# Separate evacuation lane for the key and gate tiles, and another first head, in a hybrid-layer kernel on Trainium2

## The chip, the cores and the metric

The kernel runs on one core of one Trainium2 chip. The metric is the device time of one launch in microseconds (us). The kernel before takes 2522.82 us, the median of 3 runs (2521.14 to 2523.16). Differences under some 0.2% (5 us) are about what such runs cannot tell apart.

The core has a matrix engine (TensorE, PE in the profile, with PEld its weight loads), three elementwise engines (VectorE or DVE, ScalarE or ACT, GpSimd or POOL) and queues that issue transfers (SP). Each engine runs its own instructions strictly in the order in which they were written, and engines wait for each other by semaphores.

## The reference

512 tokens of width 1024 go through two layers of one kind (gated delta rule, sliding-window attention, gated MLP) and one of another kind (a state-space branch and a pooling branch), which the change leaves alone. Of a layer of the first kind this much matters:

```python
h = rmsnorm(x, pre_mix_g)
proj = h @ w_in
(dn_q, dn_k, dn_v, dn_z, dn_b, dn_a, sw_q, sw_k, sw_v, gate_a, gate_b) = split(proj)

# delta rule, 8 heads of 128, chunks (here 128 rows on the chip)
qkv = silu(causal_conv4(concat(dn_q, dn_k, dn_v)))   # four taps
q = l2norm(q) * 128**-0.5;  k = l2norm(k)
beta = sigmoid(dn_b)
g = cumsum(-exp(a_log) * softplus(dn_a + dt_bias))   # the decay, by chunk
L = strict(beta * k @ k.T * exp(g_i - g_j));  T = inverse(1 + L)
a = (q @ k.T) * exp(g_i - g_j)
# scan over chunks: state, output o, then
o = rmsnorm(o, norm_g) * silu(dn_z)

# attention rotates the first 16 of each head's 64 columns of q and k
y = sigmoid(gate_a) * (o @ w_up_dn) + sigmoid(gate_b) * (attention @ w_up_sw)
x = x + rmsnorm(y @ w_o, post_mix_g)
x = x + rmsnorm(square(relu(rmsnorm(x, pre_mlp_g) @ w_ff1)) @ w_ff2, post_mlp_g)
```

## The kernel before

**Tiles and parts.** Everything is kept transposed: 128 features in the partitions, 512 tokens in the columns. A weight matrix is walked in tiles of 128 output features; `layer_tiles` lists them: `ab` (the 16 rows of decay and beta), then the gate tiles `z0` and `z1`, then for each head `q`, `k`, `v` and, from head 2 on, `z`; then the attention's tiles, the gates, the projections, the MLP. A tile is eight parts (`("mm", tile, part)`) of three matmuls each: weights and activations are split into a rounded high and a low rest, and high x high, low x high and high x low are summed in PSUM (`products`, L933 to L935). Each tile of weights is loaded by SP, split by ACT into the high (`split_high`, L899, two halves) and by POOL into the low (`split_low`, L906, two halves). Two wide slots take the split weights by turns; a slot comes free when the tile that used it has been multiplied. Each layer begins with four tiles whose weights were split ahead, in the slots 0 and 1 and in two extra ones that lie in room used later by others. In the second layer these four are multiplied part by part in turns; in the first only the first two.

**Evacuation.** The first four tiles write PSUM banks 2 to 5, every later one bank 0 or 1 by turns, so a tile can start only when the tile two before it was read once by its `scale` (DVE, L1693: product times the row's normalizer, into `tmp`). For q, k and v there follow `tap3` (ACT, L1430: times the last tap's weight), `tap2`, `tap1`, `tap0` (DVE, L1696: the shifted taps are added), `tanh` (ACT, L1432) and `silu` (DVE, L1699); for z only `scale`, `tanh`, `silu` (L1693, L1436, L1701). All tiles but those of the MLP's first product go through these stages as one chain, counted by one semaphore, `tile_stage`, with one buffer `tmp`.

**The decay (`G`).** `turn` (PE, L1815) transposes the result of `ab`; a chain of 15 small steps on DVE (L1483 to L1496) and ACT (L1320 to L1328: tanh, abs, exp, ln, exp) makes g; `cumsum` (PE, L1819, L1820) adds it up; `copyc`, `diff` (DVE), `exps` (ACT, L1330 to L1332) and `nbeg` end it.

**Each head's own matrices (`D`).** `square` (ACT, L1338) of q waits for all of the head's q, k, v; `sums` (PE, L1831), `qscale` (DVE, L1513), `turnk` (PE, L1838: k is transposed), `ksum` (ACT, L1341), `root` (ACT, L1345, L1346), `copyk` (ACT, L1355: k times a decay, into `kd`), `turnv` (PE, L1838 again), `recip` and `dscale` (DVE, L1516, L1518), `copyv` (ACT, L1358, into `vb`), `rows` (PE, L1834), `diff` (DVE, L1522), `exps` (ACT, L1348, L1349), `qdec` (POOL, L1272), `gramk` and `gramq` (PE, L1836) and the masks. All of `D` shares one bank of PSUM, so it is one strict chain across the engines. `A` inverts (L1855, L1859 on PE), `B` scans.

**Rotary tables (`R`).** In the first layer only, 16 steps (DVE, L1096 to L1101 and L2288 to L2291; ACT, L1467, L1468) make the sine and cosine tables. They begin when `k` of head 0 has been evacuated.

**The order.** `layer_order` writes the order of each engine: it has a list of chains, what each step needs (`needs`), which engine does it, and a planned length (`micros`, scaled by `slack1`). `ordered` always takes the step that can start first by these lengths. The result, `L_ORDERS`, is then read by each engine's program, which writes its own steps in that order. So a change of a chain, of a need or of a planned length moves instructions on every engine.

## Time and profile before

| | |
|---|---|
| median of 3 runs | 2522.82 us |
| profiled execution, its own time | 2522.34 us |
| its span, first to last instruction | 2520.6 us |
| PE busy in it | 2421.3 us, 96% |
| DVE, ACT, POOL busy | 50%, 42%, 46% |
| granted TensorE clock, mean | 0.977 |

In rows of waits the first name is what waited, the name behind the arrow what it waited for, and then come the total, the number of times and the longest, in us. In rows in order of time the columns are start, duration, engine, line, operation, what it writes and reads and its shape, and in brackets the idle time of the engine before it and what ended it. The 2.4 GHz clock of TensorE is shown as 1.00 and 1.2 GHz as 0.50. Layer one begins near 15 us, its successor near 1072 us.

### The profile page before, as it was taken

To read this page: it belongs to the slowest core of one execution; us is meant where nothing else is said; L and a number is where in the kernel's file an instruction comes from. 1 tells how busy PE (TensorE), PEld (TensorE's weight loads), DVE (VectorE), ACT (ScalarE), POOL (GpSimd) and SP (SyncE) were. 2 spreads that over 40 slices of the span, in tenths; PEclk is the share of its full clock that TensorE was granted. 3 is DMA by queue.
4 is the path that set the end of the run, shared out by engine and by line. 5 is a ranking of instruction groups with operands and counts; after the bars stand their busy time and mean duration, and the time that the engine had idled before them with its cause. 6 is when DMAs were issued, how large, how long until landed. Compare 5 with 4: busy or idle time off the path is not lost.

```text
span 2520.6 us, 35035 instructions
## 1 busy us (share of the span) xinstructions
PE 2421.3 (96%) x13972; PEld 1924.9 (76%) x13972; DVE 1256.3 (50%) x2172; ACT 1057.5 (42%) x2254; POOL 1153.6 (46%) x848
## 2 busy tenths in 40 slices
PE   7999999999999999988999999999999999799998
PEld 5777777777778888766878777787777788677886
DVE  4767654673341111266667446633485511566453
ACT  5565643543343323345566434443533332313342
POOL 4323323334666555543323233356665564433464
PEclk9999999999999999989999999999999999878999
DMA  4211112122223233311111122223234332362232
GB/s 138 67 51 51 51 43 68 59 76 76 92 76 100 92 94 99 101 59 51 58 44 60 43 68 67 68 84 110 66 111 122 121 98 93 99 185 85 93 99 75
DMA packets 76514, 207.47 MB, mean 82 GB/s; under 512 B 16704, under 2 KB 27712, under 8 KB 75840
## 3 DMA queue, kind: packets, MB, share of 16 engines
q1 hardware_dynamic: 76352, 205.24, 25.9%
q8 instruction: 110, 1.80, 0.3%
q14 instruction: 52, 0.43, 0.1%
HBM read 194.72 MB, written 10.49 MB: 81 GB/s over the span
## 4 chain that ended last, share of the span: by engine, by line
PE 81%; DVE 9%; ACT 4%; POOL 2%; issue 2%; DMA 1%; SPq 0%; DVEq 0%; ACTq 0%; POOLq 0%
PE ps L933 23%; PE ps L935 21%; PE ps L934 21%; PE ps L1855 2%; PE ps L1859 2%; PE ps L1908 1%; PE ps L1920 1%; PE ps L1836 1%; POOL wL L906 1%; ACT wH L899 1%; PE ps L1914 1%; ACT prob L1404 1%; DVE ctw L1143 1%; DVE ctmp L1143 1%; PE ps L1885 1%
## 5 line engine op out<-in xcount | busy, mean ns | idle before, releaser
L906 POOL TENSOR_TENSOR wL<-raw,wH 128x512 fp32r<-128x512 f32 x660 | 901.7, 1388 | 1143.7 <-ACT wH L899 1143.4
L899 ACT ACTIVATE wH<-raw 128x512 fp32r<-128x512 f32 x660 | 379.7, 624 | 769.5 <-PE ps L935 766.1
L933 PE MATMUL ps<-hH,wH 128*128 128x512 f32 x1592 | 667.5, 419 | 11.0 <-DVE tmp L1693 8.8
L935 PE MATMUL ps<-hH,wL 128*128 128x512 f32 x1592 | 633.4, 398 | 0.0
L934 PE MATMUL ps<-hL,wH 128*128 128x512 f32 x1592 | 631.2, 396 | 0.0
L933 PEld LDWEIGHTS ps<-hH,wH 128*128 128x128 f32 x1592 | 303.7, 191 | 82.8 <-issue 22.7
L935 PEld LDWEIGHTS ps<-hH,wL 128*128 128x128 f32 x1592 | 303.4, 191 | 67.8
L934 PEld LDWEIGHTS ps<-hL,wH 128*128 128x128 f32 x1592 | 304.9, 191 | 54.9 <-issue 0.7
L933 PE MATMUL ps<-OH,wH 128*128 128x512 f32 x576 | 230.8, 401 | 4.9 <-DVE acc L1722 1.8
L935 PE MATMUL ps<-OH,wL 128*128 128x512 f32 x576 | 227.8, 396 | 0.0
L934 PE MATMUL ps<-OL,wH 128*128 128x512 f32 x576 | 227.8, 395 | 0.0
L933 PE MATMUL ps<-SH,wH 128*128 128x512 f32 x436 | 172.6, 396 | 0.0
L935 PE MATMUL ps<-SH,wL 128*128 128x512 f32 x436 | 172.5, 396 | 0.0
L934 PE MATMUL ps<-SL,wH 128*128 128x512 f32 x436 | 172.4, 395 | 0.0
L933 PEld LDWEIGHTS ps<-OH,wH 128*128 128x128 f32 x576 | 108.2, 188 | 36.7 <-issue 9.2
L1724 DVE TENSOR_TENSOR acc<-acc,ps 128x512 f32<-128x512 f32 x48 | 33.0, 687 | 202.0 <-PE ps L935 202.0
L935 PEld LDWEIGHTS ps<-OH,wL 128*128 128x128 f32 x576 | 108.2, 188 | 26.1
L934 PEld LDWEIGHTS ps<-OL,wH 128*128 128x128 f32 x576 | 108.3, 188 | 24.8
L933 PEld LDWEIGHTS ps<-SH,wH 128*128 128x128 f32 x436 | 81.9, 188 | 20.2 <-issue 0.4
L934 PEld LDWEIGHTS ps<-SL,wH 128*128 128x128 f32 x436 | 81.9, 188 | 19.8
L935 PEld LDWEIGHTS ps<-SH,wL 128*128 128x128 f32 x436 | 81.9, 188 | 19.7
L1404 ACT ACTIVATE prob<-prob,small 128x256 f32<-128x256 f32 (+1 forms) x128 | 59.9, 469 | 61.6 <-DVE small L1640 61.6
(405 smaller groups left out, 3461.8 us busy)
## 6 DMA issues: line engine op xcount, KB each, us to landing
raw<-w SPq DMA_DIRECT2D x345, 512.0 KB, 3.5
mats<-matsD SPq DMA_DIRECT2D x4, 1408.0 KB, 6.6
x<-xT SPq DMA_DIRECT2D x8, 256.0 KB, 5.8
matsD<-Cd SPq DMA_DIRECT2D x8, 256.0 KB, 2.7
matsD<-wide SPq DMA_DIRECT2D x4, 512.0 KB, 3.6
mats<-lagsD SPq DMA_DIRECT2D x32, 64.0 KB, 6.4
outT<-acc SPq DMA_DIRECT2D x8, 256.0 KB, 2.2
matsD<-tab SPq DMA_DIRECT2D x8, 128.0 KB, 1.9
```

The lines of the kernel that those rows point to most:

```text
L899: act.activation(weights_at(slot)[0][:, k, :], raw[:, n % RAW, k, :], ACT.Copy).then_inc(high_done, 1)
L906: pool.tensor_tensor(low[:, k, :], raw[:, n % RAW, k, :], high[:, k, :].bitcast(F32), ALU.subtract).then_inc(low_done, 1)
L933: pe.matmul(out, wh, rH[:, t, :], start=(t == 0), stop=False)
L934: pe.matmul(out, wh, rL[:, t, :], start=False, stop=False)
L935: mm = pe.matmul(out, wl, rH[:, t, :], start=False, stop=(t == depth - 1))
L1143: return v.tensor_tensor(o, a, b, ALU.mult)
L1404: act.activation(prob[:, i, a:], prob[:, i, a:], ACT.Exp, bias=nm4[:, i:i + 1], accum_out=den[:, i:i + 1])
L1724: ins = v.tensor_tensor(acc[:, i % 8, :], acc[:, i % 8, :], b, ALU.add)
L1836: ins = pe.matmul(psD[:, 0, cc], k[:, cc], (k if s == "gramk" else q)[:, cc], start=True, stop=True)
L1855: ins = pe.matmul(psA[b, 0, cc], lt[b, c, b], Xi[b, i, :], start=True, stop=True)
L1859: ins = pe.matmul(second_half(psA[b, 0, cc], n), Pm[b, i, :], second_half(xb[b, i, :], n), start=True, stop=True)
L1885: ins = pe.matmul(psS[e], XT[SLOT[h]][:, c, :], vb[SLOT[h]][:, 0, :] if c == 0 else rr, start=True, stop=True)
```

## The change

It has five pieces.

- The tiles of a layer now begin `ab`, `q0`, `k0`, `v0`, `z0`, and every head has its `q`, `k`, `v`, `z` in that order. The table of slots follows.
- The tiles `k` and `z` go through their stages as a chain of their own, with a semaphore (`key_stage`) and a buffer (`tmp2`) of their own. `q`, `v` and all others stay in the old one.
- `D`'s `square` waits for the head's q alone, `turnk` for its k, `turnv` for its v. New needs say what shares the bank in head 0: `sums` comes behind the decay's `copyc`, `copyk` behind its `exps`; `copyv` of head 0 waits for the product of `z0`, whose weights lie where `vb` will.
- The rotary steps begin behind the last `D` step of head 4 instead of behind `k` of head 0.
- The planned length of the decay's steps becomes 1.0 on ACT, 0.5 on PE and 0.3 on DVE, where it was 0.25 for all.

```diff
 def layer_tiles():
-    out = [("ab", 0), ("z", 0), ("z", 1)]
+    out = [("ab", 0)]
     for h in range(HEADS):
-        out += [("q", h), ("k", h), ("v", h)] + ([("z", h)] if h > 1 else [])
+        out += [("q", h), ("k", h), ("v", h), ("z", h)]
...
-    special = {("ab", 0): 2, ("z", 0): 3, ("z", 1): 0, ("q", 0): 1, ("k", 0): 2, ("f1", 0): 2, ("f1", 1): 3, ("f1", 4): 2}
+    special = {("ab", 0): 2, ("q", 0): 3, ("k", 0): 0, ("v", 0): 1, ("z", 0): 2, ("f1", 0): 2, ("f1", 1): 3, ("f1", 4): 2}
...
-E = Count([(t, e_stages(t)) for t in LT_TILES if t[0] != "f1"])
+E = Count([(t, e_stages(t)) for t in LT_TILES if t[0] not in ("f1", "k", "z")])
+K = Count([(t, e_stages(t)) for t in LT_TILES if t[0] in ("k", "z")])
...
     if kind == "G":
-        return 0.25
+        return {"act": 1.0, "pe": 0.5, "vector": 0.3}[engine_of(e)]
...
         if (kind, j, s) == ("R", 0, "cast"):
-            out = [e_last(("k", 0))]
+            out = [last("D", 4)]
...
+            if (j, s) == (("k", 0), "scale"):
+                out.append(("E", ("ab", 0), "scale"))
...
         if kind == "D":
-            if s == "square":
-                out.append(e_last(("v", j)))
+            if s in ("square", "turnk", "turnv"):
+                out.append(e_last(({"square": "q", "turnk": "k", "turnv": "v"}[s], j)))
+            if (j, s) == (0, "sums"):
+                out.append(("G", 0, "copyc"))
+            if (j, s) == (0, "copyk"):
+                out.append(("G", 0, "exps"))
+            if (j, s) == (0, "copyv"):
+                out.append(("mm", L_AT["z", 0], PARTS - 1))
...
-    chains += [[("E", t, s) for t in LT_TILES if t not in up for s in e_stages(t)], pieces(LT_TILES, groups)]
+    chains += [[("E", t, s) for t in LT_TILES if t not in up and (t[0] in ("k", "z")) == keys for s in e_stages(t)] for keys in (True, False)]
+    chains.append(pieces(LT_TILES, groups))
...
-        tmp = sb("tmp", [P, SEQ])
+        tmp, tmp2 = sb("tmp", [P, SEQ]), sb("tmp2", [P, SEQ])
...
+            def lane(tile):
+                return (key_stage, K) if tile[0] in ("k", "z") else (tile_stage, E)
...
-                                        pe.wait_ge(tile_stage, E.before(freed, e_freed(freed)) + 1)
+                                        stage, count = lane(freed)
+                                        pe.wait_ge(stage, count.before(freed, e_freed(freed)) + 1)
...
+                            if s == "turnk":
+                                pe.wait_ge(key_stage, K.end(("k", h)))
+                            if s == "turnv":
+                                pe.wait_ge(tile_stage, E.end(("v", h)))
+                            if s == "sums" and h == 0:
+                                pe.wait_ge(gate_stage, G.before(0, "copyc") + 1)
```

The lines of the kernel after are some 13 to 26 higher than before (L933 is L946, L1693 is L1712, L1696 is L1715).

**First place: PE, second layer, around the decay's sum.** The two matmuls that read `small` are `cumsum`, `L933` to `L935` (then `L946` to `L948`) are one part of a tile, the one that reads `sq` is `sums` of head 0. Before:

```order
L935 MATMUL ps<-hH,xwL_98 128x512
L1819 MATMUL ps<-small,cst 128x32
L1820 MATMUL ps<-small,cst 128x32
L933 MATMUL ps<-hH,wH 128x512
L934 MATMUL ps<-hL,wH 128x512
L935 MATMUL ps<-hH,wL 128x512
```

After:

```order
L948 MATMUL ps<-hH,wL 128x512
L1839 MATMUL ps<-small,cst 128x32
L1840 MATMUL ps<-small,cst 128x32
L946 MATMUL ps<-hH,wH 128x512
L947 MATMUL ps<-hL,wH 128x512
L948 MATMUL ps<-hH,wL 128x512
L1857 MATMUL ps<-cst,sq 128x1 x4
```

Between `turn` and `cumsum` there stood 10 parts (30 rows) and now stand 22 (66 rows); in the first layer it is 10 before and 21 now. `sums` of head 0 stood 24 parts behind `cumsum` and now follows it by one part.

**Second place: DVE, second layer, from the first evacuation on.** `tmp` as output is a `scale` (the buffer's number is left out, so two of them stand for `tmp` and `tmp2`), `zs`, `qs` and `ks` are a gate tile, q and k, `small` are steps of the decay. Before:

```order
L1693 TENSOR_TENSOR U<-ps,rstd 16x512
L1693 TENSOR_TENSOR tmp<-ps,rstd 128x512
L1483 COPY small<-ps 128x64
L1485 TENSOR_SCALAR small<-small 128x32
L1487 TENSOR_TENSOR small<-small,par 128x32
L1701 SCALAR_TENSOR_TENSOR zs_57<-zs_57,tmp 128x512
L1490 TENSOR_SCALAR small<-small 128x32
```

After:

```order
L1712 TENSOR_TENSOR U<-ps,rstd 16x512
L1712 TENSOR_TENSOR tmp<-ps,rstd 128x512 x2
L1500 COPY small<-ps 128x64
L1715 SCALAR_TENSOR_TENSOR qs_49<-tmp,par,qs_49 128x511
L1715 SCALAR_TENSOR_TENSOR qs_49<-tmp,par,qs_49 128x510
L1502 TENSOR_SCALAR small<-small 128x32
L1715 SCALAR_TENSOR_TENSOR ks_53<-tmp,par,ks_53 128x511
L1504 TENSOR_TENSOR small<-small,par 128x32
L1715 SCALAR_TENSOR_TENSOR ks_53<-tmp,par,ks_53 128x510
L1507 TENSOR_SCALAR small<-small 128x32
```

The decay's small steps now stand between the taps of q and k of head 0, where two short gate tiles stood before. Ahead of the last step that `cumsum` needs (L1496, after: L1513) DVE now has 16 wide evacuation steps, where it had 6.

**Third place: ACT, second layer, head 0 from its `ksum` to its `copyv`.** `sums_of` is `ksum`, `kd` is `copyk`, `vb` is `copyv`, `wH<-raw` is a `split_high`. Before:

```order
L1341 ACTIVATE sums_of,scal<-ps 128x128 x4
L1432 ACTIVATE tmp<-qs_50 128x512
L1345 ACTIVATE scal<-scal 128x4
L1346 ACT_TABLE_LOAD
L1346 ACTIVATE scal<-scal,cst 128x4
L1355 ACTIVATE kd_74<-ps,small 128x128 x4
L1430 ACTIVATE ks_54<-tmp,par 128x512
L899 ACTIVATE wH<-raw 128x512 x2
L1358 ACTIVATE vb_81<-ps,scal 128x128 x4
```

After:

```order
L1359 ACTIVATE scal<-scal,cst 128x4
L1449 ACT_TABLE_LOAD
L1449 ACTIVATE tmp<-qs_50 128x512
L1368 ACTIVATE kd_74<-ps,small 128x128 x4
L1449 ACTIVATE tmp<-ks_54 128x512
L909 ACTIVATE wH<-raw 128x512 x2
L1447 ACTIVATE vs_52<-tmp,par 128x512
L909 ACTIVATE wH<-raw 128x512 x2
L1373 ACTIVATE vb_81<-ps,scal 128x128 x4
```

The `tanh` of q of head 1, with its table load, now stands between `root` and `copyk`; two weight splits stand between `copyk` and `copyv`, where one stood before.

## Rows read from the trace of the kernel before

**Rows 1.** The page: busy times, and the chain that ended last.

```profile
PE 2421.3 (96%) x13972; PEld 1924.9 (76%) x13972; DVE 1256.3 (50%) x2172; ACT 1057.5 (42%) x2254; POOL 1153.6 (46%) x848
...
PE 81%; DVE 9%; ACT 4%; POOL 2%; issue 2%; DMA 1%; SPq 0%; DVEq 0%; ACTq 0%; POOLq 0%
```

**Rows 2.** Stretches: span, busy time of each engine (instructions), granted clock, DMA.

```profile
36.00:103.00 67.00, 59.66 (x313) 47.68 (x314) 51.84 (x86) 36.13 (x71) 26.08 (x19) 0.97 0.23 71
103.00:430.00 327.00, 322.15 (x2720) 254.98 (x2719) 196.16 (x426) 173.59 (x422) 106.63 (x79) 0.99 0.16 51
1102.00:1160.00 58.00, 47.76 (x207) 37.11 (x207) 37.67 (x58) 29.81 (x62) 23.09 (x17) 0.94 0.23 73
1160.00:1500.00 340.00, 335.25 (x2840) 266.16 (x2839) 204.79 (x451) 178.61 (x431) 110.00 (x83) 1.00 0.17 52
```

**Rows 3.** PE in order of time, first layer's opening.

```profile
36.57 0.39 PE L1815 MATMUL ps<-cst,U 16*128 16x16 f32 x4 [0.60 <-DVE U L1693]
...
45.26 0.41 PE L1819 MATMUL ps<-small,cst 128*128 128x32 f32 x2 [1.20 <-DVE small L1496]
...
77.86 0.55 PE L1838 MATMUL ps<-cst,vs 128*128 128x128 f32 x3 [1.90 <-ACT kd L1355]
...
87.12 0.47 PE L933 MATMUL ps<-hH,wH 128*128 128x512 f32 x1 [1.29 <-DVE tmp L1693]
...
96.78 0.42 PE L1859 MATMUL ps<-XB,Pm 64*64 64x32 f32 x8 [1.41 <-DVE Pm L1555]
```

**Rows 4.** PE in order of time, second layer's opening.

```profile
1102.80 0.39 PE L1815 MATMUL ps<-cst,U 16*128 16x16 f32 x4 [0.58 <-DVE U L1693]
...
1113.99 0.41 PE L1819 MATMUL ps<-small,cst 128*128 128x32 f32 x2 [3.62 <-DVE small L1496]
...
1129.19 0.47 PE L933 MATMUL ps<-hH,wH 128*128 128x512 f32 x1 [1.90 <-DVE tmp L1693]
...
1152.59 0.63 PE L933 MATMUL ps<-hH,wH 128*128 128x512 f32 x1 [2.83 <-DVE tmp L1693]
```

**Rows 5.** Three stretches at the half clock, columns as in rows 2.

```profile
98.00:101.40 3.40, 3.40 (x11) 2.82 (x11) 2.56 (x5) 0.71 (x2) 0.00 (x0) 0.51 0.50 154
1115.20:1118.60 3.40, 3.40 (x9) 2.67 (x8) 2.67 (x7) 1.10 (x4) 0.00 (x0) 0.50 0.00 0
1152.80:1156.20 3.40, 2.92 (x8) 1.81 (x8) 2.48 (x2) 0.85 (x2) 2.98 (x3) 0.51 0.30 93
```

**Rows 6.** DVE in order of time, second layer's opening.

```profile
1105.04 0.18 DVE L1485 TENSOR_SCALAR small<-small 128x32 f32<-128x32 f32 x1 [1.53 <-ACT small L1320]
1105.25 1.19 DVE L1487 TENSOR_TENSOR small<-small,par 128x32 f32<-128x32 f32 x1
1106.36 1.83 DVE L1701 SCALAR_TENSOR_TENSOR zs<-zs,tmp 128x512 f32<-128x512 f32 x1
```

**Rows 7.** ACT in order of time, second layer.

```profile
1110.66 1.28 ACT L1326 ACT_TABLE_LOAD   x1
1111.96 0.23 ACT L1326 ACTIVATE small<-small 128x32 f32<-128x32 f32 x1
...
1142.47 1.14 ACT L1355 ACTIVATE kd<-ps,small 128x128 f32<-128x128 f32 x4
```

**Rows 8.** The page's groups of the weight splits: busy time, mean ns of one.

```profile
L906 POOL TENSOR_TENSOR wL<-raw,wH 128x512 fp32r<-128x512 f32 x660 | 901.7, 1388 | 1143.7 <-ACT wH L899 1143.4
L899 ACT ACTIVATE wH<-raw 128x512 fp32r<-128x512 f32 x660 | 379.7, 624 | 769.5 <-PE ps L935 766.1
```

**Rows 9.** DVE groups by shape, 20 to 420 us: busy us, mean ns | idle before.

```profile
L1693 DVE TENSOR_TENSOR tmp<-ps,rstd 128x512 f32<-128x512 f32 x34 | 23.3, 685 | 8.1 <-PE ps L935 7.6
L1696 DVE SCALAR_TENSOR_TENSOR qs<-tmp,par,qs 128x510 f32<-128x510 f32 x8 | 6.7, 843 | 0.2
```

**Rows 10.** DVE groups of the rotary steps, 59 to 82 us, first and last.

```profile
L2288 DVE TENSOR_SCALAR kr<-kc 128x512 f32<-128x512 f32 x2 | 1.7, 858 | 0.0
...
L1100 DVE TENSOR_SCALAR ropeS<-ropeS,cst 128x512 f32<-128x512 f32 x1 | 0.5, 487 | 1.7 <-ACT ropeC L1468 1.7
```

34 lines of the change are left out of this document (20 added, 14 removed).

## The prediction

> **What bounds the kernel now.** I read the page first: the engine shares and the chain that ended last. PE is busy 96% of the span and carries 81% of that chain, the next engine 9% [rows 1]. The number of matmuls does not change, so all there is to win or lose is time in which PE stands still, some 99 us of 2520.6, and time at the half clock. Then I looked where PE stands still, by stretches: the change touches only the head stages of the two hybrid layers. In the first layer PE idles 7.3 us of the first 67 and then only 4.9 us of 327; in the second 10.2 of 58 and then 4.8 of 340 [rows 2]. So the losses sit in the opening, before the heads' pipeline has filled. Last I read PE in order of time there, to see what each wait waited for. In the first layer: `cumsum` for the decay's last small step 1.20, `turnv` of head 0 for `copyk` 1.90, a tile for the bank that a `scale` had to free 1.29, the inverse's second product 1.41 [rows 3]. In the second: `cumsum` 3.62, tiles for their bank 1.90 and 2.83 [rows 4]. Waits under 0.6 us are left out. After the longer ones the granted clock shows 0.5 for 3.4 us: behind the group that ends with 1.41 in the first layer, behind the 3.62 and with the 2.83 in the second [rows 5]. The 1.90 at 1129 alone is not followed by such a stretch. A stretch with PE busy throughout loses half of 3.4, 1.7 us, the last one, with 2.92 busy, 1.5.
>
> **What goes.** First layer: 1.20 + 1.90 + 1.29 + 1.41 + 1.7 = 7.5 us. Second: 3.62 + 1.90 + 2.83 + 1.7 + 1.5 = 11.6. In all 19.1, if every one of these goes and nothing comes. The waits for the result of `ab` (0.60 and 0.58) stay: its `scale` and `turn` stand where they stood.
>
> **`cumsum`, the decay's chain.** A part takes 0.7 us: PE began `turn` at 1102.80 and was through the 10 parts behind it at 1113.99 less the wait of 3.62, 1110.4 [rows 4]; some 0.3 of these 7.6 us are `turn` itself. Now 22 parts lie there, so PE comes to `cumsum` 1103.1 + 22 x 0.7 = 1118.5. The chain, though, gets slower, since it now shares DVE with the taps of q, k and v of head 0. On DVE 16 wide steps and 7 small ones stand between the first `scale` (1102.0) and the chain's last step: 5 scales at 0.69, 8 taps and 3 silus at 0.75 (the row's mean is 0.84, with its stretched ones) [rows 9], together 11.7; the small ones at 0.2, and three of them at the 1.2 that they take now and then [rows 6], 4.4; two short waits for ACT, 0.4. That gives 1118.5, the same moment. I take 0.4 us of wait in place of 3.62, and the same for the first layer, where 21 parts lie between (due at 51.6, chain ready near 52.1, with the table loads of ln and exp on ACT before it). Bounds: 0 and 3.6.
>
> **Banks.** A tile waits for the `scale` of the tile two before. With one lane this `scale` stood behind all seven stages of the tile before; the 1.29, 1.90 and 2.83 are just that. Now k and z on one side, q and v on the other alternate, so a bank is freed by the other lane than the one still busy. In the openings I find each `scale` ahead of its due time by 1 us or more, so 0.
>
> **`D` of head 0 in the second layer, where I expect new waits.** `sums` can now start when q is done, so `turnk` comes at about 1122.2. ACT then has `ksum` (1.1), tap3 of k of head 1 (0.7), `root` with its table load (1.8), tanh of q of head 1 with another load (1.9), and only then `copyk` (1.14 [rows 7]): it ends near 1129.6. PE has `v1` behind `turnk` and is at `turnv` by 1128.7: 0.9 of wait. Behind `copyk` on ACT stand a tanh (0.6) and then the split of `z1`, whose slot has been free since 1123. Its first half is high at 1130.8 and low 1.3 later [rows 8], and PE wants it at 1130.0: 2.0. `rows` then waits for `copyv`, which stands behind a tap3 and another split (0.7 + 1.25): ready at 1134.3 against 1133.4: 0.9. In sum 3.8 new, which is between 0 (ACT gets there sooner) and 6. In the first layer the same walk has `copyk` ending 0.4 ahead of `turnv` and `rows` just in time; I take 0.4 for it. For the inverse, the first product and the second now have two parts between them instead of none, 1.4 us against the 1.41 that was missing: 0.
>
> **Rotary steps.** Ten groups of DVE steps, 18 instructions, 11.8 us [rows 10] (the first and the last of the ten), and two ACT steps with a table load. They leave a stretch in which DVE was busy 51.8 of 67 us and enter one in which it is busy 60% [rows 2]. Each can put a small step of the scan or the inverse off by 0.5 to 1.7. PE's products there are placed with slack; I take 1.0, between -1.0 (the opening is freed further) and 4.
>
> **Sum.** -19.1 + 0.8 (both cumsum) + 3.8 + 0.4 + 1.0, and 1.7 for one half-clock stretch that the 3.8 brings along = -11.4 us. The profiled execution took 2522.34 around its span of 2520.6, 0.5 below the median of 2522.82; so 2511.
>
> **Two rules weighed.** ACT switches its function table in 1.28 us, and the next function starts 0.02 later [rows 7]. The Trainium skill (ScalarE: Activation LUTs, "What ACT_TABLE_LOAD costs") adds a drain of about 1.38 us to each switch; for the four switches of the decay's chain and `root` that now stand ahead of `copyk` it would be an estimate of 5 us more and would eat half the gain. The row has no such drain, so I leave it out.
> DVE's wide steps take 0.69 or, at times, 1.83, its small ones 0.18 or 1.19 [rows 6]; the longer ones fall where POOL is splitting weights. The Trainium skill (SBUF — State Buffer, "Who interferes with whom") says that of a DVE operation with two inputs in SBUF and a GpSimd operation the later one is blocked for the whole of the other. The first rival is what this would do here, with its numbers from rows.
>
> **Rival one, 18%: the gain of the second layer does not come.** The splits of three tiles, six halves of 1.39 [rows 8], run in just the stretch into which the taps move. The walk above has three stretched steps. With six, at 1.0 each (1.19 against 0.18, 1.83 against 0.69) [rows 6], the decay's chain is 3 us later, `cumsum` waits 3.4 as before and the half clock follows, 1.7; `D` shifts with PE and keeps its 3.8. The total is -11.4 + 3.0 + 1.7 = -6.7, 2516; with a second such stretch 2518. For: the small steps at 1.2 in the chain now. Against: only some of the steps are hit.
>
> **Rival two, 14%: paid back later.** PE reaches the filled pipeline 11 us sooner, and if another engine bounded the rest it would just wait there: 2521 to 2523. Against it: DVE and ACT are busy 60% and 53% of the 327 us, and PE waits 1.5% [rows 2].
>
> **Rival three, 9%, slower: the new order is too tight in the filled pipeline.** From head 2 on the order on all engines is new. k's chain now waits its turn on DVE behind the inverse and the scan, and a late `scale` of k or z holds PE at the next tile. Its price is that of such a wait now, 1.29 to 1.90 [rows 3, 4]. Once in each of the 16 heads at 1.6 it is 25.6: 2511 + 25.6 = 2537. It makes the kernel slower than before from 0.8 us per head. For: the late `scale` of k in the order; against: the stretch waits 4.8 us in all now [rows 2] with a planner of the same lengths.
>
> **How the numbers follow.** Forecast 59%, own range 2506 to 2516. The low end of all is every wait gone, 2522.8 - 19.1 = 2504. At the high end I let rival one and half of rival two in, 2522, and leave out rival three. This kernel's runs cannot tell less than about 0.2%, 5 us, from no change. Faster by more: the forecast nearly whole (0.57), two thirds of rival one (0.12): 0.69. Slower: 0.09 of rival three. The rest, 0.22, is the same.
>
> **What the profile will show.** Right: PE's wait at `cumsum` under 1 us in both layers, no tile waiting over 1 us for a `scale` in the openings, no half clock before 110 us in the first layer; new waits at `turnv` and at the first matmul of `z1` in the second, with ACT's split of `z1` right before the latter. Wrong: `cumsum` still waiting 3 us (rival one), PE idle growing in 103 to 430 and 1160 to 1500 by what the openings gain (rival two), or by more, with tiles waiting for `scale` (rival three).

## The result: 0.9% faster, about twice the forecast

| | before | after |
|---|---|---|
| device time, median | 2522.99 us (4 runs) | 2499.95 us (4 runs, 2497.98 to 2501.46) |
| profiled execution, its own time | 2522.34 us | 2497.98 us |
| its span | 2520.6 us | 2496.2 us |
| granted TensorE clock, mean | 0.977 | 0.978 |

The ratio is 0.9908, 95% interval 0.9893 to 0.9924. The forecast was 2511, range 2504 to 2522: the sign was right, the size was not, and the time lies below the range. Two more sets of runs of the changed kernel, on two chips, gave 2505.54 us (before: 2522.01) and 2502.83 us (before: 2523.26). So the gain is 23.0, 16.5 and 20.4 us, against 11.4 forecast. Of all the executions in this document two fell into a slower state of the chip, one of `no_lane` (2971.74) and one of the kernel before beside it (4441.54); the intervals leave them out, and the medians 2533.41 and 2524.41 would be 2533.28 and 2524.21 without them.

The page of the kernel after, to be held against [rows 1]: PE busy in us, and the chain.

```profile
PE 2414.7 (97%) x13972; PEld 1921.3 (77%) x13972; DVE 1266.1 (51%) x2172; ACT 1047.8 (42%) x2248; POOL 1152.0 (46%) x848
...
PE 83%; DVE 8%; ACT 4%; POOL 2%; issue 2%; DMA 1%; SPq 1%; DVEq 0%; ACTq 0%; POOLq 0%
```

PE idles 81.5 us of the span instead of 99.3. The stretches of the kernel after that answer to [rows 2], and two stretches at the half clock that answer to [rows 5]. Columns: stretch, its length, busy us (instructions) of PE, PEld, DVE, ACT, POOL, then granted clock and DMA.

```profile
34.00:103.00 69.00, 67.59 (x424) 53.38 (x423) 50.61 (x88) 41.92 (x92) 27.08 (x21) 1.00 0.23 70
103.00:430.00 327.00, 324.11 (x2668) 257.77 (x2668) 209.18 (x449) 169.85 (x417) 108.15 (x80) 0.99 0.18 54
1090.00:1148.00 58.00, 53.77 (x298) 42.67 (x298) 46.92 (x76) 33.98 (x76) 23.31 (x17) 0.94 0.22 73
1148.00:1488.00 340.00, 338.22 (x2801) 268.05 (x2801) 209.31 (x451) 175.43 (x437) 115.02 (x85) 1.00 0.17 54
28.70:32.10 3.40, 3.40 (x12) 2.74 (x11) 0.07 (x1) 0.00 (x0) 0.00 (x0) 0.50 0.50 154
1120.90:1127.70 6.80, 5.55 (x15) 4.51 (x16) 6.70 (x9) 3.47 (x9) 5.80 (x4) 0.50 0.23 78
```

In the first layer's opening PE now idles 1.4 us instead of 7.3, in the second's 4.2 instead of 10.2. The filled stretches idle 2.9 instead of 4.9 and 1.8 instead of 4.8, which the forecast did not have.

PE in order of time, the longer waits that are left in the head stages, against [rows 3, 4]. The line numbers are those of the kernel after: L1835 is `turn`, L1839 `cumsum`, L1864 `turnv`.

```profile
320.43 0.66 PE L1864 MATMUL ps<-cst,vs 128*128 128x128 f32 x4 [1.48 <-ACT kd L1368]
...
1107.87 0.41 PE L1839 MATMUL ps<-small,cst 128*128 128x32 f32 x2 [0.56 <-DVE small L1513]
...
1119.77 0.65 PE L1864 MATMUL ps<-cst,vs 128*128 128x128 f32 x4 [1.37 <-ACT kd L1368]
...
1122.15 0.80 PE L946 MATMUL ps<-hH,wH 128*128 128x512 f32 x1 [1.73 <-POOL wL L916]
```

The first layer's waits of 1.20, 1.90, 1.29 and 1.41 [rows 3] are all gone, and so are the second's tile waits of 1.90 and 2.83 [rows 4]. At `cumsum` 0.56 stands for 3.62. The waits for the result of `ab` stay, at 0.56 and 0.57. The two new waits, at `turnv` and at the first matmul of `z1`, are there as forecast. The 1.48 at 320.43 is new too and was not forecast: `turnv` of a later head now waits in the first layer's filled stage, where the kernel before had 1.54 at a `sums`. In the two later profiles of this kernel (after2 and after3 below) the wait at `turnv` of the second layer is 0.77 in both, the one at `z1` 1.73, and a third of 1.38 and 1.40 stands at `gramk` of head 0, which this profile does not have.

### The profile page after: what moved, and what is told of

Read it like the earlier page. It is cut to its first block, busy times and chain, and to the rows that moved or that the text cites. A ratio compares the mean times of both kernels' runs of the same rounds, so it can differ in the third digit from the quotient of the medians.

```text
span 2496.2 us, 35065 instructions
## 1 busy us (share of the span) xinstructions
PE 2414.7 (97%) x13972; PEld 1921.3 (77%) x13972; DVE 1266.1 (51%) x2172; ACT 1047.8 (42%) x2248; POOL 1152.0 (46%) x848
## 4 chain that ended last, share of the span: by engine, by line
PE 83%; DVE 8%; ACT 4%; POOL 2%; issue 2%; DMA 1%; SPq 1%; DVEq 0%; ACTq 0%; POOLq 0%
PE ps L946 24%; PE ps L948 22%; PE ps L947 22%; PE ps L1881 2%; PE ps L1885 2%; PE ps L1934 1%; PE ps L1946 1%; PE ps L1862 1%; ACT wH L909 1%; POOL wL L916 1%; PE ps L1940 1%; DVE ctw L1156 1%; ACT prob L1419 1%; DVE ctmp L1156 1%; PE ps L1911 1%
## 5 line engine op out<-in xcount | busy, mean ns | idle before, releaser
L946 PE MATMUL ps<-hH,wH 128*128 128x512 f32 x1592 | 667.0, 419 | 3.9 <-DVE mixed L2177 2.2
L948 PE MATMUL ps<-hH,wL 128*128 128x512 f32 x1592 | 631.9, 397 | 0.0
L946 PEld LDWEIGHTS ps<-hH,wH 128*128 128x128 f32 x1592 | 303.1, 190 | 74.0 <-issue 11.3
L948 PEld LDWEIGHTS ps<-hH,wL 128*128 128x128 f32 x1592 | 302.7, 190 | 67.6
L946 PE MATMUL ps<-OH,wH 128*128 128x512 f32 x576 | 230.8, 401 | 4.9 <-DVE acc L1741 1.8
L948 PE MATMUL ps<-OH,wL 128*128 128x512 f32 x576 | 227.8, 396 | 0.0
L946 PE MATMUL ps<-SH,wH 128*128 128x512 f32 x436 | 172.6, 396 | 0.0
L948 PE MATMUL ps<-SH,wL 128*128 128x512 f32 x436 | 172.5, 396 | 0.0
L946 PEld LDWEIGHTS ps<-OH,wH 128*128 128x128 f32 x576 | 108.2, 188 | 36.8 <-issue 9.2
L948 PEld LDWEIGHTS ps<-OH,wL 128*128 128x128 f32 x576 | 108.2, 188 | 26.0
L946 PEld LDWEIGHTS ps<-SH,wH 128*128 128x128 f32 x436 | 81.9, 188 | 20.2 <-issue 0.4
L948 PEld LDWEIGHTS ps<-SH,wL 128*128 128x128 f32 x436 | 81.9, 188 | 19.7
```

What stands on the lines that cost most here:

```text
L946: pe.matmul(out, wh, rH[:, t, :], start=(t == 0), stop=False)
L948: mm = pe.matmul(out, wl, rH[:, t, :], start=False, stop=(t == depth - 1))
```

## Where the 24.4 us of the two profiles went

To compare the same work I cut both traces at the same tile parts. Columns as above. In the fence of before one stretch at the half clock stands first. Of the cuts, the first row is parts 1 to 96 of the first layer, the second 97 to 352 (the end of its heads), the third the rest up to the second layer, then the same three cuts of that layer (128, 352 and 672 parts in), and last the layer of the other kind. First the kernel before, then the kernel after, and then the kernel after in another execution (run after3 below).

```profile
26.40:33.20 6.80, 6.80 (x25) 6.01 (x25) 0.35 (x2) 1.77 (x3) 2.13 (x2) 0.50 0.26 80
...
8.46:108.16 99.70, 88.67 (x444) 67.00 (x444) 64.80 (x105) 54.07 (x108) 44.59 (x32) 0.95 0.29 99
108.16:432.60 324.44, 319.59 (x2684) 253.23 (x2681) 195.09 (x422) 169.61 (x410) 107.27 (x79) 0.99 0.16 52
432.60:1051.17 618.57, 612.03 (x2905) 488.00 (x2904) 209.65 (x338) 235.12 (x491) 326.25 (x246) 0.99 0.27 85
1051.17:1182.32 131.15, 114.60 (x617) 88.00 (x616) 79.95 (x129) 64.01 (x133) 55.72 (x40) 0.93 0.21 68
1182.32:1476.44 294.12, 290.37 (x2512) 230.56 (x2513) 176.47 (x392) 156.68 (x380) 92.28 (x70) 1.00 0.16 51
1476.44:1750.52 274.08, 273.12 (x1443) 213.06 (x1442) 148.18 (x258) 115.56 (x288) 122.59 (x89) 1.00 0.24 78
1750.52:2507.12 756.60, 719.11 (x3355) 581.92 (x3353) 374.25 (x518) 254.88 (x434) 402.86 (x288) 0.96 0.34 104
```

```profile
8.42:101.34 92.92, 87.71 (x497) 65.62 (x497) 58.44 (x97) 54.10 (x114) 43.87 (x32) 0.98 0.32 105
101.34:420.82 319.48, 316.79 (x2632) 252.33 (x2629) 202.65 (x430) 165.22 (x402) 106.49 (x79) 0.99 0.18 53
420.82:1039.59 618.77, 612.20 (x2905) 488.20 (x2904) 209.62 (x338) 235.09 (x491) 326.04 (x246) 0.99 0.28 85
1039.59:1166.32 126.73, 116.71 (x661) 90.30 (x660) 88.23 (x140) 65.65 (x137) 56.35 (x40) 0.93 0.22 71
1166.32:1456.73 290.41, 288.80 (x2479) 229.09 (x2478) 175.77 (x383) 150.80 (x376) 93.16 (x69) 1.00 0.17 52
1456.73:1729.47 272.74, 271.78 (x1431) 211.95 (x1430) 147.72 (x256) 114.42 (x284) 122.49 (x89) 1.00 0.26 78
1729.47:2482.69 753.22, 716.89 (x3354) 580.72 (x3353) 375.80 (x518) 254.88 (x434) 401.54 (x288) 0.96 0.35 104
```

```profile
101.82:421.27 319.45, 316.74 (x2632) 252.37 (x2629) 202.57 (x430) 165.12 (x402) 106.49 (x79) 0.99 0.17 53
...
1039.81:1166.81 127.00, 115.98 (x661) 89.47 (x660) 87.75 (x140) 65.62 (x137) 56.27 (x40) 0.95 0.22 70
1166.81:1458.81 292.00, 290.38 (x2480) 230.34 (x2478) 175.69 (x383) 150.78 (x376) 93.19 (x69) 0.99 0.16 52
...
1731.65:2488.69 757.04, 719.74 (x3354) 582.17 (x3353) 375.06 (x518) 254.85 (x434) 402.51 (x288) 0.95 0.34 104
```

| parts | forecast | measured, idle in it | after3 |
|---|---|---|---|
| layer one, 1 to 96 | -6.7 | -6.8, -5.8 | -7.0 |
| 97 to 352 | +1.0 | -5.0, -2.2 | -5.0 |
| 353 to 1152 | 0 | +0.2, 0 | 0.0 |
| layer two, first 128 | -5.7 | -4.4, -6.5 | -4.2 |
| next 224 | 0 | -3.7, -2.1 | -2.1 |
| next 320 | 0 | -1.3, 0 | -1.2 |
| the third layer | 0 | -3.4, -1.2 | +0.4 |

(Idle is length less PE busy of the same row.) So of the 24.4 us 3.4 lie in a layer whose program the change leaves alone, and in after3 that layer is 0.4 longer than before: they are taken as scatter. The head stages give 21.2, in after3 19.5, and that is the gain. The openings came out close to the sum, in part by luck, since 53 and 44 more matmuls lie in them now. The filled stages did not: they gave 8 to 10 us where I had +1.0. The cut hides a part: the 53 more matmuls lie in the first layer's first 96 parts (497 against 444) and 52 fewer lie behind, so the heads' work has moved forward into the opening. What one can read without that cut is the whole head stage: in the first layer idle fell by 8.0 us and the length by 11.7, in the second by 8.7 and 9.5 (in after3 by 8.0 and 12.0, and by 7.6 and 7.5).

## Experiments

Each time is the median of several runs beside runs of the kernel before on the same chip (medians of before in the four batches: 2522.65 beside u_lane, u_order, u_rotary and u_gates; 2522.01 beside after2, u_needs, o_lane and v_copyk; 2523.26 beside after3, u_both, o_rotary and o_gates; 2524.41 beside the three pairs). "Layer one" and "layer two" are the lengths of parts 1 to 352 and of the 672 parts from the start of layer two, from one profiled execution of each kernel. That execution is not always near the median: it took 2512.40 for u_gates, whose six runs lie between 2503.65 and 2513.18, and 2524.92 for o_rotary, the longest of twelve.

| run | what it is | us | ratio, 95% | layer one | layer two |
|---|---|---|---|---|---|
| | before | 2522.99 | | 424.1 | 699.4 |
| | after | 2499.95 | 0.9893 to 0.9924 | 412.4 | 689.9 |
| after2 | after, again | 2505.54 | 0.9915 to 0.9942 | 413.6 | 691.8 |
| after3 | after, again | 2502.83 | 0.9906 to 0.9932 | 412.2 | 691.8 |
| u_lane | after, one lane | 2522.93 | 0.999 to 1.0008 | 424.1 | 698.7 |
| u_order | after, old tile order | 2509.93 | 0.9927 to 0.996 | 415.2 | 696.4 |
| u_needs | after, old needs of `D` | 2514.99 | 0.9952 to 0.9977 | 414.8 | 696.1 |
| u_rotary | after, rotary early | 2507.17 | 0.9918 to 0.9949 | 415.2 | 690.2 |
| u_gates | after, old decay lengths | 2507.25 | 0.9921 to 0.9956 | 420.8 | 690.6 |
| u_both | after without the last two | 2512.27 | 0.9945 to 0.9969 | 419.4 | 690.7 |
| o_lane | before + lane | 2546.64 | 1.0076 to 1.0104 | 425.4 | 708.9 |
| o_rotary | before + rotary late | 2520.69 | 0.9979 to 0.9999 | 426.7 | 701.0 |
| o_gates | before + decay lengths | 2520.29 | 0.9977 to 0.9999 | 424.3 | 697.9 |
| l_order | before + lane + order | 2513.73 | 0.9949 to 0.9975 | 419.5 | 696.3 |
| l_needs | before + lane + needs | 2507.81 | 0.9917 to 0.9945 | 415.3 | 691.2 |
| no_lane | before + order + needs | 2533.41 | 1.0024 to 1.0053 | 428.1 | 705.0 |
| v_copyk | after + two needs | 2503.13 | 0.99 to 0.9929 | 413.6 | 690.8 |

What profiles of the same code differ by: layer two is the same program in before and o_rotary, 699.4 and 701.0, and in after, after2, after3 and u_rotary, 689.9, 691.8, 691.8 and 690.2. So some 2 us or less of such a length says nothing. Of the times, the intervals of u_rotary and u_gates overlap with those of after2 and after3; that they are slower than the kernel after rests on the mean of its three sets.

### One piece taken out of the kernel after

**One lane again (u_lane).**

```diff
-E = Count([(t, e_stages(t)) for t in LT_TILES if t[0] not in ("f1", "k", "z")])
-K = Count([(t, e_stages(t)) for t in LT_TILES if t[0] in ("k", "z")])
+E = Count([(t, e_stages(t)) for t in LT_TILES if t[0] != "f1"])
+K = E
...
-                return (key_stage, K) if tile[0] in ("k", "z") else (tile_stage, E)
+                return (tile_stage, E)
...
-                            raw_out = tmp2 if kd_ in "kz" else tmp
+                            raw_out = tmp
```

> The changed kernel with all of k and z back in the one chain, one semaphore and one buffer; the tiles' order, the finer needs, the late rotary steps and the decay's lengths stay. Theory one: the waits of tiles for a scale come back in the openings (1 to 3 us each, three to four of them, with a half-clock stretch), 2506 to 2510. Theory two: also in the filled stages, 103 to 430 us and its twin, where idle time grows by 3 us or more each; 2512 or more. If neither, within 3 us of 2500.

The whole gain is gone (2522.93). PE around head 0 in the second layer:

```profile
1118.96 1.12 PE L1864 MATMUL ps<-cst,ks 128*128 128x128 f32 x4 [0.25 <-DVE scal L1530]
1126.17 1.11 PE L1864 MATMUL ps<-cst,vs 128*128 128x128 f32 x4 [6.09 <-ACT kd L1368]
```

`turnk` and `turnv` follow each other with no tile part between, and PE stands 6.09 us for `copyk`. The clock is at its half level for 10.2 us around it, from 1118.9, before PE stops, to 1129.1. In the kernel after the same two stand at 1111.54 and 1119.77, with nine parts (27 matmuls) between, and the wait is 1.37. With one lane the next tile's `scale` on DVE comes at 1125.84, behind the last stage of v, and the tile that would take its bank can't be put between. (That this is why the planner left the place empty is read from the order, and no run shows it by itself.) In the first layer, which loses 11.7 us, the opening has no such wait; the filled stage idles 8.5 us instead of 2.7, most of it at `turnv`, which waits for the last step of v (1.44, 1.19, 0.46), and at the inverse (1.65). So theory two came true, with more than it expected.

**Old tile order (u_order).**

```diff
-    out = [("ab", 0)]
+    out = [("ab", 0), ("z", 0), ("z", 1)]
     for h in range(HEADS):
-        out += [("q", h), ("k", h), ("v", h), ("z", h)]
+        out += [("q", h), ("k", h), ("v", h)] + ([("z", h)] if h > 1 else [])
...
```

> The changed kernel with the old order of tiles (ab, z0, z1, q0, ...) and its table of slots; two lanes, the finer needs, the late rotary steps and the decay's lengths stay. Theory one (the gain is the opening's, and comes from giving the decay's chain 21 to 22 parts of tile work ahead of its sum and starting the first head earlier): the sum is again due 10 parts after turn, PE waits there over 2 us in the second layer and over 0.5 in the first, and the time is 2510 or more, at least 10 us above the changed kernel's 2500. Theory two (the lane carries most, in the filled stages too): under 2505.

2509.93, near theory one's number, but not by its mechanism: `cumsum` waits 0.54 us in the second layer and not at all in the first, since the planner, with the decay's new lengths, still puts 19 parts ahead of it. The opening of the second layer is even shorter (119.2 us for its first 128 parts against 126.7), but the heads then end later than the tiles and PE waits 1.93 at attention's first score: the 320 parts behind take 286.0 us with 8.8 idle, against 272.7 with 1.0. The rest of the 8.8 is seven waits of 0.39 to 1.39 for attention's masks (`prob`, DVE) over the next 140 us.

**Old needs of `D` (u_needs).**

```diff
-                out.append(e_last(({"square": "q", "turnk": "k", "turnv": "v"}[s], j)))
+                out += [e_last((t, j)) for t in ({"square": "qkv"}.get(s, ""))]
...
```

> The changed kernel, but a head's square waits for all of its q, k and v again. Theory one (the gain is the lane's and the order's): D starts some 5 to 8 us later in each head, the planner moves it back by that, and the pipeline has the slack: within 3 us of the changed kernel. Theory two (the early start of D gives the filled stages their slack): D's products are late there as before, idle time in the two filled stages together grows by 4 us or more, 2505 or more.

2514.99, theory two, in the same picture as u_order: the heads end late. DVE starts attention's first rotation at 1471.35, when POOL has split the last heads' output, and the first score waits for that chain. In the second layer:

```profile
1477.97 0.93 PE L1935 MATMUL ps<-kk,rstdp 64*128 64x128 f32 x8 [1.92 <-DVE rstdp L1633]
```

**Rotary steps early again (u_rotary).**

```diff
-            out = [last("D", 4)]
+            out = [e_last(("k", 0))]
```

> The changed kernel with the rotary steps starting behind k of head 0 again. The prediction priced the move at 1.0 us lost in the filled stage and counted the relief of the opening in the waits there. Theory one: the steps' 11.8 us of DVE sit in the first layer's opening, where DVE was busy 51.8 of 67 us; they cost 3 to 6 us there and give 1 back: 2503 to 2505. Theory two: the opening now has room for them, and their move was worth nothing: 2499 to 2501. Nothing changes in the second layer in either.

2507.17, 4.4 us over the mean of the three sets of the kernel after and 1.6 over after2, so its size is not settled. In the profile the first layer's heads take 2.8 us more than in the kernel after (415.2 against 412.4; 1.6 more than in after2), all of it in the opening: parts 97 to 352 take 319.4 or 319.5 in all of them. PE there:

```profile
68.47 0.65 PE L1860 MATMUL ps<-cst,small 128*128 128x128 f32 x4 [0.73 <-ACT vb L1373]
...
77.32 1.16 PE L1862 MATMUL ps<-ks 128*128 128x128 f32 x8 [1.99 <-POOL qd L1285]
```

In the kernel after these two waits are 0.31 and 0.41. So where the filled stage takes up the rotary steps no price shows, and the opening gains some 2 us of idle time.

**The decay's old planned lengths (u_gates).**

```diff
-        return {"act": 1.0, "pe": 0.5, "vector": 0.3}[engine_of(e)]
+        return 0.25
```

> The changed kernel with the planned length 0.25 for every step of the decay, as before. Theory one: the planner again believes the chain to be short and puts its sum well ahead of the point where the chain is ready; PE waits there 2 to 4 us in each layer, with a half-clock stretch in the second: 2505 to 2510. Theory two: the planned lengths only shuffle small steps; within 2 us of 2500.

2507.25. `cumsum` waits again, in both layers:

```profile
49.13 0.41 PE L1839 MATMUL ps<-small,cst 128*128 128x32 f32 x2 [2.27 <-DVE small L1513]
...
1109.80 0.41 PE L1839 MATMUL ps<-small,cst 128*128 128x32 f32 x2 [2.48 <-DVE small L1513]
```

The first layer loses 8.4 us in this profile, one of the longer executions: 2.27 at `cumsum`, and 6.8 us of half clock at 50.5 that the kernel after does not have, are part of it. The second loses nothing beyond its scatter: there no wait at `turnv` or `z1` is over 0.6 us once `cumsum` waits, though `gramk` waits 1.74.

**Both of the last two out (u_both),** the edits of u_rotary and u_gates together.

> The changed kernel with two pieces taken out: rotary steps early again and the decay's old planned lengths. What is left is lane, new tile order and the needs. Additive: undone singly they gave 2507.2 each, some 4 us over the changed kernel, so 8 us, 2511 to 2513 (ratio 0.996). Rival, order, lane and needs make one unit that bears the gain and the two others correct the same thing (DVE's load in the opening): 2507 to 2509, no more than one of them undone. Second rival, without both the opening of the first layer falls together as with the lane alone (a wait of 4 us at gramk or gramq, half clock behind): over 2518.

2512.27, the additive theory: 9.4 us over after3 on the same chip, about what the two cost singly (some 4 us each on the mean of the three measurements of after, 2502.8).

### One piece put into the kernel before

**The lane alone (o_lane):** the kernel before with `K`, `key_stage` and `tmp2` as in the diff. The needs of head 0 that name what shares its bank, and what must be done before `copyv`, are in it as well.

> The kernel before with nothing changed but the second lane (k and z by themselves, with a semaphore and a buffer of their own); old tile order, old needs (but that D of head 0 names its wait for the decay's copy, which it met anyway), early rotary steps, old lengths of the decay. Theory one (the lane is necessary, and enough for most): the waits of tiles for a scale go, 1.29 in the first layer and 1.90 and 2.83 in the second, with one half-clock stretch, and small ones in the filled stages: 2510 to 2514; the wait at the decay's sum stays. Theory two (the lane is necessary but does little by itself, since the short gate tiles ahead of q0 and the decay's early sum still hold the opening): 2517 to 2522.

24.6 us slower, where both theories had it faster. PE in the first layer, and at attention's first score:

```profile
93.33 1.16 PE L1863 MATMUL ps<-ks 128*128 128x128 f32 x8 [2.21 <-POOL qd L1285]
98.67 1.65 PE L1863 MATMUL ps<-qs,ks 128*128 128x128 f32 x6 [4.18 <-DVE XB L1554]
...
441.13 0.93 PE L1935 MATMUL ps<-kk,rstdp 64*128 64x128 f32 x8 [1.90 <-DVE rstdp L1633]
```

`gramk` and `gramq` of head 0 stand one behind the other without a part between, and the clock is at its half level for 13.7 us, from 94.0 to 107.7. Then the heads end behind the tiles in both layers: the stretch behind layer one's heads, which no other variant changes by more than 1 us, takes 626.0 us instead of 618.6, and layer two's takes 283.3 instead of 274.1. `square` still waits for all of q, k and v, which now end in two chains; that these are out of step and so make the heads late is argued and not measured. The third layer takes 3.9 us more in this profile than in that of before, about its scatter.

**Rotary steps late, alone (o_rotary).**

```diff
-            out = [e_last(("k", 0))]
+            out = [last("D", 4)]
```

> The kernel before with one thing new: the rotary steps begin behind the last D step of head 4. Theory of additive pieces: undoing this in the changed kernel cost 1.7 to 2.8 us in the first layer's head stage (415.2 us against 412.4 and 413.5), so alone it should give the same, 2520 (ratio 0.999), with PE's wait at the inverse (1.41 at 96.8 us) or at the bank gone. Rival, pieces that only pay together: alone the move frees DVE in an opening that is bound by the one chain and not by DVE, and loads the stage behind; no change or up to 4 us slower, 2522 to 2526, with PE idle between 103 and 430 us above the 4.9 us of before. The prediction's own term for the move was +1.0.

2520.69; the interval just excludes no change, but the first layer of its profile, the longest of its executions, is 2.6 us longer, so nothing is settled beyond that it is small. PE in that opening:

```profile
85.15 0.77 PE L933 MATMUL ps<-hH,wH 128*128 128x512 f32 x1 [3.21 <-DVE tmp L1693]
```

The inverse's 1.41 is gone, but the tile's wait for its bank, 1.29 before, has grown to 3.21, and the filled stage idles 8.2 us instead of 4.9: part of what the rival expected.

**The decay's lengths alone (o_gates).**

```diff
-        return 0.25
+        return {"act": 1.0, "pe": 0.5, "vector": 0.3}[engine_of(e)]
```

> The kernel before with one thing new: the planned lengths of the decay's steps (1.0, 0.5, 0.3 instead of 0.25), so cumsum is placed later. Additive: undoing it in the changed kernel brought back waits of 2.27 and 2.48 us at cumsum and cost about 4 us; alone it should give 3.6 + 1.2 of wait and one half-clock stretch, 6 us, 2516 (ratio 0.9975), with the wait at cumsum under 1 us in both layers. Rival, only together: in the old order sums of head 0 is far behind anyway, and the planner pushes head 0's matrices later still, so the waits at the bank (1.9 and 2.8 us in the second layer) grow by what cumsum gives: 2521 to 2525.

2520.29, short of the additive 2516. In the second layer the 3.62 at `cumsum` shrinks to 0.29, and then:

```profile
1118.69 0.47 PE L933 MATMUL ps<-hH,wH 128*128 128x512 f32 x1 [1.21 <-DVE tmp L1693]
...
1133.32 1.05 PE L1831 MATMUL ps<-cst,sq 128*128 128x1 f32 x8 [1.80 <-ACT sq L1338]
...
1150.72 0.77 PE L933 MATMUL ps<-hH,wH 128*128 128x512 f32 x1 [2.84 <-DVE tmp L1693]
```

Half of what `cumsum` gives comes back as a wait for `square` that was not there before; of the two waits for a bank [rows 4] one is 0.7 shorter and the other as long as it was, but with 6.8 us of half clock around it where there were 3.4.

### Pairs

What was open at this point was which piece turns the lane from a loss of 24.6 us into a gain. The kernels are the kernel after with the edits of u_both and, besides, one whose diff is above: that of u_needs (l_order is lane and tile order), that of u_order (l_needs is lane and needs) or that of u_lane (no_lane is tile order and needs).

> The kernel before with the second lane and the new order of the tiles (first head ahead of the gate tiles, extra slots to match); square still waits for all of q, k and v, decay's lengths and rotary steps as before. Theory, the order makes the lane pay: with q, k, v of head 0 first and z in turns, head 0's matrices come early enough, and the split needs only add the 9 us that undoing them cost: 2521 to 2523 (2512.3 + 9.5), heads no longer ending behind the tiles, so no wait of 1.9 us at attention's first score. Rival, only order and needs together: 2530 to 2547, the score wait of 1.9 us and 7 us more idle behind the heads as with the lane alone.

> The kernel before with the second lane and the split needs (square waits for q, turnk for k, turnv for v), gate tiles z0 and z1 still first. Theory, the order makes the lane pay: without it 2530 to 2547, waits of 2 to 4 us behind head 0's matrices in the first layer. Rival, the needs make it pay (the waits of 4.18 and 2.21 us there come from a chain that begins only when k, v of the head are done in lanes that no longer stand in step): 2519 to 2523, that is the 2512.3 of lane, order and needs plus the 7 us that undoing the order cost.

> The kernel before with the new tile order and the split needs, one lane. Additive: the changed kernel without its lane ran at the time of before (2522.9), rotary and decay's lengths were worth 3 us each there at most, so 2524 to 2529. Rival, the 20 us that undoing the lane cost stand only against the other two pieces: then without them it should be near 2512 + 20 = 2532 or more. A wait of some 6 us at turnv in the second layer, as in the changed kernel without its lane, should stand in its profile in either case.

Either piece does it. Lane and order give -10.7 us, still with 1.93 at attention's first score; lane and needs give -16.6, nearly as much as all five pieces. Both together, u_both, give -11.0, less than the needs alone with the lane (the two intervals just touch). Without the lane, order and needs lose 9.0. The second layer of no_lane has `turnv` right behind `turnk` as u_lane has, with a longer wait, this time for the last step of v:

```profile
1137.64 1.09 PE L1864 MATMUL ps<-cst,vs 128*128 128x128 f32 x4 [8.12 <-DVE vs L1718]
```

And l_needs waits 2.91 us at `cumsum` in the second layer, which the lengths would take away, but nowhere over 0.6 us behind it in that opening.

Adding the lengths and the late rotary to l_needs is u_order, 2509.93: no gain, where they give 9.4 on top of u_both. For l_order and l_needs both theories missed, by 7 and 11 us, since I had added up what the pieces cost singly; for no_lane the rival held. Pieces do not add up here.

### The two new waits taken away

**v_copyk** adds two needs, so that the tanh of q1 stands behind `copyk` of head 0 and the tanh of k1 behind the split of `z1`.

```diff
+            if (j, s) == (("q", 1), "tanh"):
+                out.append(("D", 0, "copyk"))
+            if (j, s) == (("k", 1), "tanh"):
+                out.append(("split_high", L_AT["z", 1], None))
```

> The changed kernel with two more needs told to the planner alone: tanh of q of head 1 behind copyk of head 0, and tanh of k of head 1 behind the split of z1. On ACT in the second layer copyk then follows root after one split, without the tanh and its table load, and the split of z1 stands ahead of it. The first layer's order stays as it is. If the waits of 1.37 and 1.73 that the changed kernel has at turnv and at z1 are this queue's on ACT, both fall under 0.5 and the half-clock stretch of 6.8 us behind them goes or halves: 3 to 6 us under the changed kernel. If they only move (the planner's new order puts other work late), within 2 us of it.

2503.13 against 2505.54 on the same chip, not to be told apart. The waits at `turnv` and `z1` are gone, and smaller ones have come: 0.90 at `rows`, 0.72 at `gramk` and 0.91 at `gramq`. The 3 to 6 us of the first theory did not come.

**The kernel after again, twice.**

> The changed kernel itself once more, on the same chip as the three others of this set. It is the yardstick for the ablations, whose times were taken against the kernel before on another chip. If the gain of 23 us holds everywhere, 2498 to 2502; the state-space stage, which no kernel here touches, took 753 us in its profile and 756 to 760 in the others, so a share of the gain may be scatter: then 2501 to 2504.

> The changed kernel again, as the yardstick of this chip. Theory that the gain is 16 to 23 us and the difference between the two earlier figures (2499.95 and 2505.54) is scatter of the chips and of stages that the change leaves alone: 2500 to 2506, ratio 0.991 to 0.993, first layer's head stage 412 to 414 us, second's 689 to 692. Rival: the two figures differ by something in the head stages; then these stages should differ by more than 2 us from both profiles seen.

2505.54, above what was expected, and 2502.83, within it. Head stages of 1105.4 and 1104.0 us against 1102.3 in the first profile and 1123.5 before: their gain is 18.1 to 21.2 us.

## Why the prediction was wrong

**The bound was right, and half of the place.** PE's idle time in the head stages was what there was to win, but not in the openings alone. All seven waits that the sum let go went, but for 0.56 at `cumsum`, where I had left 0.4.

**"Waits under 0.6 us are left out", and the filled stages at +1.0: this step failed.** I counted 5.8 us of waits in the first layer and 8.35 in the second, all in the openings, and took the rest as fixed. The head stages of before idle 15.9 and 21.3 us (rows of the kernel before above), and after 7.9 and 12.6. The first layer lost 8.0 us of idle time where my sum had 5.0 (5.8 less 0.8 of new waits), the second 8.7 where it had 4.15 (8.35 less 0.4 and 3.8). Of the 9.8 us by which the head stages beat the forecast 7.5 are such idle time, 1.4 are busy time of PE (less half clock) and 1.0 is the rotary term; in after3 it is 8.1, made up of 6.5, 0.6 and 1.0.

What I read past in the kernel before was not only short. PE in the filled stages (a fourth, 1.14 at `gramk` at 1412.41, is like the last):

```profile
331.06 1.05 PE L1831 MATMUL ps<-cst,sq 128*128 128x1 f32 x8 [1.54 <-ACT sq L1338]
...
1182.32 0.47 PE L933 MATMUL ps<-hH,wH 128*128 128x512 f32 x1 [0.76 <-DVE tmp L1693]
...
1185.93 0.38 PE L1836 MATMUL ps<-ks 128*128 128x128 f32 x1 [1.36 <-POOL qd L1272]
```

In the second layer these went: its filled stage has one wait over 0.3 left, 0.73 at `gramk`, and 1.25 us of short waits in its opening are gone. In the first layer the 1.54 only changed its place (1.48 at `turnv`), and the six waits of 0.37 to 0.61 of its filled stage became one of 0.39; besides, the 0.8 of new waits in its opening did not come. I had looked at [rows 2], seen only 4.9 and 4.8 us there, and priced this place as one that would lose. The variants show what holds these waits down. Parts 97 to 352 idle 4.8 to 8.5 us in all five profiles without the lane (before, o_rotary, o_gates, no_lane, u_lane), and 2.4 to 3.8 in those with it, but for u_order and u_needs, with 4.9 and 5.1. So the lane lowers them, but beside the late rotary steps and the new lengths it does so only with both the order and the needs. That it works by freeing a bank from either lane is argued, not measured by itself.

**Rotary, "I take 1.0": it measured 0.** The filled stage paid nothing for the steps (319.4 us with and without them). Their relief of the opening, some 2 us of idle time by u_rotary, was in my sum among the waits that go.

**The half clock, 1.7 kept.** In the first layer 6.8 us of half clock at 26.4 became 3.4 at 28.7, ahead of everything the change does there; after2 has 6.8 again. That is chance and not in the sum, but it breaks a sign that I had named: "no half clock before 110 us in the first layer" overlooked the 6.8 us at 26.4 in the kernel before. The stretch at 98, which the sign meant, is gone. In the second layer the profile of after has 6.8 us behind the two new waits instead of the 3.4 that I gave them, and nothing behind `cumsum`; after2 and after3 have 3.4 us in all, from 1112.2 and 1110.6, a few us behind the 0.54 and 0.56 at `cumsum`, and nothing behind the new waits. So the place of a stretch was not mine to forecast, and its size was right in two of three.

**The decay's chain: right.** I had 15.7 us from `turn` to the last step and 22 parts of 0.7 beside it; it took 16.1 (1091.50 to 1107.62) and PE was through at 1107.31. DVE in order of time, kernel after:

```profile
1092.87 3.22 DVE L1715 SCALAR_TENSOR_TENSOR qs<-tmp,par,qs 128x511 f32<-128x511 f32 x2
1096.01 1.27 DVE L1502 TENSOR_SCALAR small<-small 128x32 f32<-128x32 f32 x1
1097.20 1.84 DVE L1715 SCALAR_TENSOR_TENSOR ks<-tmp,par,ks 128x511 f32<-128x511 f32 x1
1098.96 0.18 DVE L1504 TENSOR_TENSOR small<-small,par 128x32 f32<-128x32 f32 x1
```

And POOL in the same stretch:

```profile
1092.53 5.97 POOL L916 TENSOR_TENSOR wL<-raw,wH 128x512 fp32r<-128x512 f32 x4
```

Four DVE steps start in POOL's 5.97 us and take 3.9 us more than their usual lengths (3.22 for two of 0.75, 1.27 for 0.18, 1.84 for 0.75). From 1098.96 on, when POOL has ended, each takes its short time. That is the mechanism of rival one, and it costs 3.9 us where my walk had 3.0 for it, not the 6 that the rival needed. The Trainium skill (SBUF — State Buffer, "Who interferes with whom") has the blocking for DVE operations with two inputs in SBUF, and the three taps in these rows agree. The small step of 1.27 has one input and was held up as well.

**The waits of head 0: right in the sum.** Forecast 0.9, 2.0 and 0.9 at `turnv`, `z1` and `rows`, 3.8 in all; measured 1.37, 1.73 and under 0.3. In after2 and after3 it is 0.77, 1.73, at most 0.2, and some 1.4 at `gramk`, which I did not have. ACT ahead of them, kernel after:

```profile
1116.44 0.30 ACT L1359 ACTIVATE scal<-scal,cst 128x4 f32<-128x4 f32 x1
1116.76 1.28 ACT L1449 ACT_TABLE_LOAD   x1
1118.05 0.63 ACT L1449 ACTIVATE tmp<-qs 128x512 f32<-128x512 f32 x1
```

Each function starts 0.01 us behind its load. A drain of 1.38 us for each switch, as the Trainium skill has it (ScalarE: Activation LUTs, "What ACT_TABLE_LOAD costs"), is not there; with two of them, as an estimate, `turnv` would have waited some 4 us.

**Rivals.** One did not come: the chain was ready as forecast. Two did not come: nothing was paid back, the filled stages gained. Three did not come here, but o_lane shows a near neighbour of this kernel in which it did, at 24.6 us, and u_order, u_needs and l_order a part of it: heads that end behind the tiles cost 7 to 8 us of idle time from attention's first score on. I had put the price at tiles waiting for a `scale`, and it showed elsewhere.

**The range.** Its low end was the sum of the counted waits. That is no bound while the head stages idle 37 us.

**What stays open.** Why lane and needs without the order (l_needs) do as well as they do, and whether they would do better with one of the two small pieces alone, was not tried; the orders differ from the first head on. The split of the gained length between the filled stages and the openings is one of where the heads' work lies, and no run separates it. Why each piece changes the planner's order as it does was read from the orders, not tested.

## What to carry to other kernels

Where a greedy planner writes the order, price the whole list that it makes, not the edits: here the same lane cost 24.6 us alone and gave some 20 beside the other four pieces. Take as the lower end of a range all the idle time of the stages that the change touches, short waits included, and not the sum of the long ones. The waits of 4 to 8 us in u_lane, no_lane and o_lane all stand where two dependent steps follow each other with nothing between; at such a wait look for what should have been between, and for the resource that kept it out (here, as far as the order can be read, the PSUM bank).

## What the runs showed of the hardware

- Between two executions of the same program the second layer's head stages move by 1.6 to 2.0 us (699.4 and 701.0; 689.9 and 691.8), and the third layer by 3.8 (753.2 and 757.0). About half or more of each is busy time of PE for the same matmuls (1.4, 0.9 and 2.8 us); the rest is idle time.
- The same program differs by up to 5.6 us in its median between sets of runs (2499.95, 2505.54, 2502.83) while the kernel before differed by 2.4 (2522.01 to 2524.41). One set of runs carries that much doubt beside its interval.
- The length of a half-clock stretch is not fixed, and the wait ahead of it does not tell it alone: 3.4 us behind the 3.62 at `cumsum` of before [rows 4, 5], but 10.2 with 3.58 at the same place in no_lane; 6.8 with 3.21 (o_rotary), 10.2 around 6.09 (u_lane), 13.7 with 2.21 and 4.18 (o_lane). It can begin before the long wait (u_lane, 1118.9 against 1120.1) or with no wait over 0.6 us in the 40 us ahead of it (after3, 1110.6). I had taken 3.4 for all.
